# One inference step of a hybrid encoder layer: gate tiles before branch tiles, the convolution norm one tile up, and another order in the last block

## What is computed

```
hin = rmsnorm(x, g_pre_mix);  z = hin @ w_in
q, k, v, o_gate, it, lf = parts of z          # 4 heads of 256
hm = mLSTM(q, k, v, it, lf, C0, n0, m0)       # chunked matrix memory
hm = headnorm(hm) * g_headnorm * o_gate
branch_m = hm @ w_branch_m
u = z[CA] * sigmoid(z[CB]);  cv = depthwise_conv(concat(cache, u), 31 taps)
cv = silu(layernorm(cv, ln_g, ln_b))
branch_c = cv @ w_branch_c
merged = sigmoid(z[GM]) * branch_m + sigmoid(z[GC]) * branch_c
x = x + rmsnorm(merged @ w_out, g_post_mix)
hf = square(relu(rmsnorm(x, g_pre_ffn) @ w_ff1)) @ w_ff2
x = x + rmsnorm(hf, g_post_ffn)
```

## Time and profile before

| | |
|---|---|
| median of 3 runs (lowest to highest) | 1232.36 us (1231.77 to 1232.42) |
| profiled execution: time, span | 1232.35 us, 1230.5 us |
| mean granted clock of PE | 0.991 |
| busy: PE, DVE, ACT, POOL | 1194.1, 858.1, 450.4, 22.7 us |
| read from and written to HBM | 106.13 MB, 16.83 MB |

### The profile page before, as it was taken

One profiled execution on the slowest core, in us unless ns is written; L12 is line 12 of the kernel. 1 busy time (PEld: TensorE's weight loads), 2 busy tenths in 40 slices (PEclk: granted clock), 3 DMA queues, 4 the chain that ended last, 5 costly groups with the idle time before them and its releaser, 6 DMA issues.

```text
span 1230.5 us, 19269 instructions
## 1 busy us (share of the span) xinstructions
PE 1194.1 (97%) x7512; PEld 1117.4 (91%) x7512; DVE 858.1 (70%) x1522; ACT 450.4 (37%) x667; POOL 22.7 (2%) x37
## 2 busy tenths in 40 slices
PE   8999999999999999899999999979999999999996
PEld 7998999999999988899999998778998989899895
DVE  5644469888897989788655554986666666666667
ACT  5442243124323322312147223443525336254352
POOL 2000000000000000200000000000000000000000
PEclk9999999999999999999999999989999999999998
DMA  8342352353227223322322226122313231332323
GB/s 239 108 109 83 102 156 69 104 142 94 68 86 192 60 85 93 103 70 73 86 67 68 69 73 235 69 92 97 100 56 121 69 120 38 118 120 69 103 94 130
DMA packets 147834, 123.97 MB, mean 101 GB/s; under 512 B 13615, under 2 KB 131591, under 8 KB 147762
## 3 DMA queue, kind: packets, MB, share of 16 engines
q1 hardware_dynamic: 125138, 99.03, 27.4%
q10 hardware_dynamic: 22624, 23.95, 5.9%
HBM read 106.13 MB, written 16.83 MB: 100 GB/s over the span
## 4 chain that ended last, share of the span: by engine, by line
PE 82%; DVE 10%; ACT 3%; issue 2%; DMA 1%; SPq 0%; ACTq 0%; DVEq 0%; POOLq 0%; POOL 0%
PE out L417 39%; PE out L2310 16%; PE bank L2349 9%; PE out L2349 6%; PE bank L1998 5%; DVE CV L1252 4%; PE bank L1993 3%; PE out L2260 2%; PE bank L2260 2%; DVE WK L1252 2%; DVE WL L346 1%; DVE WK L1249 1%; DMA WK<-in_x_prompt 1%; DMA xend<-in_g_post_ffn 1%; PE out L398 1%
## 5 line engine op out<-in xcount | busy, mean ns | idle before, releaser
L417 PE MATMUL out<-XH,WH 128*128 128x320 f32 (+1 forms) x1024 | 239.5, 315 | 0.0
L417 PE MATMUL out<-XL,WH 128*128 128x320 f32 (+1 forms) x1024 | 237.4, 313 | 0.0
L417 PE MATMUL out<-XH,WL 128*128 128x320 f32 (+1 forms) x1024 | 237.4, 313 | 0.0
L1252 DVE SCALAR_TENSOR_TENSOR CV<-WK,cwu,CV 128x512 f32<-128x512 f32 x480 | 226.4, 542 | 0.0
L417 PEld LDWEIGHTS out<-XH,WH 128*128 128x128 f32 x1024 | 171.4, 189 | 5.0 <-issue 4.8
L417 PEld LDWEIGHTS out<-XL,WH 128*128 128x128 f32 x1024 | 172.6, 188 | 1.8 <-issue 1.3
L417 PEld LDWEIGHTS out<-XH,WL 128*128 128x128 f32 x1024 | 172.1, 188 | 1.5 <-issue 1.3
L346 DVE TENSOR_TENSOR WL<-ST,WH 128x1024 fp32r<-128x1024 f32 x85 | 104.3, 1227 | 88.1 <-ACT WH L338 87.0
L338 ACT ACTIVATE WH<-ST 128x1024 fp32r<-128x1024 f32 x85 | 89.6, 1054 | 113.1 <-PE out L417 57.9
L768 ACT ACTIVATE WK<-out 128x640 f32<-128x640 f32 (+1 forms) x56 | 39.8, 710 | 215.8 <-PE out L417 214.4
L1249 DVE TENSOR_TENSOR WK<-out,WK 128x512 f32<-128x512 f32 (+3 forms) x82 | 44.8, 567 | 53.6 <-PE out L417 32.1
(11 more groups left out here) (252 smaller groups left out, 2137.1 us busy)
## 6 DMA issues: line engine op xcount, KB each, us to landing
ST<-in_w_in SPq DMA_DIRECT2D x65, 512.0 KB, 4.0
ST<-in_w_ff SPq DMA_DIRECT2D x32, 1024.0 KB, 5.2
WK<-in_state_mlstm_C ACTq DMA_DIRECT2D x32, 256.0 KB, 4.2
o_C_sample<-WK ACTq DMA_DIRECT2D x32, 256.0 KB, 2.7
WK<-in_x_prompt SPq DMA_DIRECT2D x8, 512.0 KB, 7.3
ST<-in_w_branch_m SPq DMA_DIRECT2D x8, 512.0 KB, 4.7
ST<-in_w_branch_c SPq DMA_DIRECT2D x8, 512.0 KB, 4.1
ST<-in_w_out SPq DMA_DIRECT2D x8, 512.0 KB, 3.6
```

What stands on the lines that cost most here:

```text
L417: last = pe.matmul(out[s][:, h, 0:H], w[:, s, kk, :], x[:, kk, h * H:(h + 1) * H], start=(m < 2), stop=(m >= len(ms) - 2))
L1252: return dve.scalar_tensor_tensor(o, x, s, y, op0, op1)
```

## The change

1. **Gates and branch m.** All eight gate tiles come first, then the eight branch tiles. The sigmoids go straight into MG (`sg` is gone), and DVE multiplies in place. `headnorm_out` moves to the middle of the third gate tile, `epilogue_gate` on DVE to the fourth, `epilogue_out` on ACT ahead of the fourth evacuation, `u_out` behind the fifth tile. The taps are five per gate tile from the second on, then four per branch tile. The last two additions of the channel sum (`lsum`) go from the first GC tile to the last branch tile. SP's loads follow; that of the second gate tile waits for one low part more, that of the third for none of its own.
2. **Convolution norm.** Each of its steps stands one tile earlier among the GC tiles: mean at r = 0, subtraction 1, squares 2, sums 3, spread and multiplication 4, Silu 5 and 6.
3. **Last block.** ACT makes both high parts of the last unit (31) ahead of the squares of the last tile f, and DVE its low parts between the last sums. `gpf` has its place in WK (that of `x2q`) and is loaded when the squares of x2 are done, ahead of the wait for p3. DVE waits for x2 by group, in `y_final`. PE does parts 0 and 1 ahead for three groups only.

```diff
-    sg = wk(off["kt"], 2 * T2).rearrange("p (a t) -> p a t", a=2)
...
-    gpf, ysq = xend[:, 0:D], xend[:, D:D + 512]
+    ysq = xend[:, D:D + 512]
...
+    gpf = x2q
@@ -603,18 +603,16 @@
-            def gates_and_branch(i):
-                for r, (w, o) in enumerate(((w_in, OFF_GM), (w_in, OFF_GM + P), (w_m, 0), (w_m, P))):
-                    more = 0 if isinstance(i, int) else {1: 1, 2: -1}.get(r, 0)
-                    load_tile(sp, N(N_GM0, 4, i) + r, w, 0, i * 2 * P + o, more)
-
-            gates_and_branch(0)
+            for r in range(4):
+                load_tile(sp, N(N_GM0 + r), w_in, 0, OFF_GM + r * P, {1: 1, 2: -1}.get(r, 0))
...
-            with sp.Fori(1, KT // 2) as i:
-                gates_and_branch(i)
+            for r in range(4, KT):
+                load_tile(sp, N(N_GM0 + r), w_in, 0, OFF_GM + r * P)
+            for r in range(KT):
+                load_tile(sp, N(N_GM0 + KT + r), w_m, 0, r * P)
@@ -661,11 +659,12 @@
+            sp.wait_ge(sem("fsq"), 5)
+            dma(gpf, a["g_post_ffn"].to_broadcast([P, D]), "gpf")
 
             products(sp, 2 * NBLK - 1, "p3")
             for c in range(5):
-                dma(x2r[:, c, :], d_x2[:, c, :], "x2_in")
-            dma(gpf, a["g_post_ffn"].to_broadcast([P, D]), "gpf")
+                dma(x2r[:, c, :], d_x2[:, c, :], f"xagain{c if c else SMP}")
@@ -989,50 +988,46 @@
-            def gates_m(i):
-                n = N(N_GM0, 8, i)
-                for g in range(2):
-                    for r in range(2):
-                        hi(n + (4 * g + r + 1))
-                        if i or g:
-                            evacuated(act, n + (4 * g - 2 + r))
-                        evac(n + (4 * g + r), two(sg[:, r, :]), ACT.Sigmoid)
-                        if i == g == r == 0:
-                            epilogue_root(HEADS - 1)
-                    hi(n + (4 * g + 3))
-                    if i == g == 0:
-                        epilogue_out(HEADS - 1)
-                    hi(n + (4 * g + 4))
-                    if i == g == 0:
-                        u_rows(HEADS - 1)
-
-            gates_m(0)
-            gates_m(1)
+            for r in range(KT):
+                hi(N(N_GM0 + r + 1))
+                if r == 3:
+                    epilogue_out(HEADS - 1)
+                if r == 4:
+                    act.wait_ge(sem("hm_lo"), HEADS)
+                if r == 5:
+                    u_rows(HEADS - 1)
+                if r == 6:
+                    act.wait_ge(sem("u_out"), 48 * HEADS)
+                evac(N(N_GM0 + r), two(MG[:, r, :]), ACT.Sigmoid)
+                if r == 0:
+                    epilogue_root(HEADS - 1)
+            for r in range(KT):
+                hi(N(N_GM0 + KT + r + 1))
...
-            act.wait_ge(sem("u_out"), 16 * 3 * HEADS)
+            act.wait_ge(sem("np_out"), 16 * HEADS)
             for r in range(KT):
                 hi(N(N_GC0 + r + 1))
-                if r == 5:
+                if r == 4:
...
-                if r == 3:
+                if r == 2:
...
-                if r >= 6:
-
-                    for kk in range(4 * (r - 6), 4 * (r - 5)):
+                if r in (5, 6):
+
+                    for kk in range(4 * (r - 5), 4 * (r - 4)):
...
-                if r == 1:
+                if r == 0:
@@ -1074,7 +1069,10 @@
             def y_hi(u, t):
 
                 raw_in(act, u)
-                w_free(act, u, "a")
+                if u == NU - 1:
+                    products(act, f_of(u - 2), "p5" if t else "p2")
+                else:
+                    w_free(act, u, "a")
@@ -1198,13 +1196,17 @@
                 y_hi(u + 1, 0)
                 p5_copy(f)
                 y_hi(u + 1, 1)
+                if b == NBLK - 1:
+                    y_hi(u + 2, 0)
+                    y_hi(u + 2, 1)
                 row1(f)
...
                 row0(2 * b + 1)
-                y_hi(u + 1, 0)
-                y_hi(u + 1, 1)
+                if b < NBLK - 1:
+                    y_hi(u + 1, 0)
+                    y_hi(u + 1, 1)
@@ -1610,18 +1612,22 @@
                     epilogue_norm(HEADS - 1)
                 if j == 1:
                     unit_params(HEADS - 1)
+                    dve.wait_ge(sem("cache_in"), 32 * HEADS)
+                if j == 3:
                     epilogue_gate(HEADS - 1)
-                    dve.wait_ge(sem("cache_in"), 32 * HEADS)
-                if j == 10:
-                    dve.wait_ge(sem("u_out"), 48 * HEADS)
-                if j % 4 >= 2:
-                    kk = 2 * (j // 4) + j % 2
+                if j >= KT:
+                    r = j - KT
                     dve.wait_ge(sem("tile_done"), val(n) + 1)
-                    evacuated(dve, n + -2)
-                    tt(two(MG[:, kk, :]), gout(n), two(sg[:, j % 2, :]), ALU.mult
+                    evacuated(dve, N(N_GM0 + r))
+                    tt(two(MG[:, r, :]), gout(n), two(MG[:, r, :]), ALU.mult
                        ).then_inc(sem(f"of{n.par % 2}"), 1)
                 if j >= 1:
-                    t = taps(HEADS - 1, t, t + 5)
+                    t = taps(HEADS - 1, t, t + (5 if j < KT else 4))
+                if j == 2 * KT - 1:
+                    dve.wait_ge(sem("conv"), 2 * TAPS * HEADS)
+                    dve.wait_ge(sem("csum"), KT - 3)
+                    V.link(tt(ln[0], ln[0], CV[:, KT - 2, :], ALU.add))
+                    tt(ln[0], ln[0], CV[:, KT - 1, :], ALU.add).then_inc(sem("lsum"), 1)
@@ -1632,16 +1638,11 @@
-                if r == 0:
-                    dve.wait_ge(sem("conv"), 2 * TAPS * HEADS)
-                    dve.wait_ge(sem("csum"), KT - 3)
-                    V.link(tt(ln[0], ln[0], CV[:, KT - 2, :], ALU.add))
-                    tt(ln[0], ln[0], CV[:, KT - 1, :], ALU.add).then_inc(sem("lsum"), 1)
-                if r == 2:
+                if r == 1:
...
-                if r == 3:
+                if r == 2:
...
-                if r == 5:
+                if r == 4:
...
-                if r >= 6:
-                    conv_remainders(4 * (r - 6), 4 * (r - 5))
+                if r in (5, 6):
+                    conv_remainders(4 * (r - 5), 4 * (r - 4))
@@ -1915,13 +1916,18 @@
+                if b == NBLK - 1:
+                    y_lo(u + 1, 0)
+                    c12(f)
+                    y_lo(u + 1, 1)
+                    g_lo(f, 1)
+                    g_lo(f, 0)
+                    return
                 c12(f)
                 g_lo(f, 1)
                 g_lo(f, 0)
                 y_lo(u + 1, 0)
                 y_lo(u + 1, 1)
-                if b == NBLK - 1:
-                    return
@@ -1961,6 +1967,7 @@
                 dve.wait_ge(sem("yg"), 2 * x + 2)
+                dve.wait_ge(sem(f"xagain{x if x else SMP}"), 32)
...
             dve.wait_ge(sem("gpf"), 16)
-            dve.wait_ge(sem("x2_in"), 16 * 5)
@@ -2211,12 +2217,13 @@
             for j in range(2 * KT):
-                if j % 4 < 2:
-                    gemm(pe, N(N_GM0 + j), XH2, XL2, gaps=[lambda: headnorm_out(HEADS - 1)] if j == 1 else ())
+                if j < KT:
+                    gemm(pe, N(N_GM0 + j), XH2, XL2, gaps=[lambda: headnorm_out(HEADS - 1)] if j == 2 else ())
                 else:
-                    gemm(pe, N(N_GM0 + j), GH, GL, rhs_ready=(lambda kk: kk == 6 and pe.wait_ge(sem("hm_lo"), HEADS))
-                         if j == 2 else None)
-                if j == 2:
+                    if j == KT:
+                        pe.wait_ge(sem("hm_lo"), HEADS)
+                    gemm(pe, N(N_GM0 + j), GH, GL)
+                if j == 4:
                     u_out(HEADS - 1, N(N_HEADS0 + PER_HEAD * (HEADS - 1)))
@@ -2240,11 +2247,11 @@
-                gemm(pe, N(N_GC0 + r), XH2, XL2, gaps=[lambda: spread("lrt", "t_lr")] if r == 5 else ())
-                if r == 1:
+                gemm(pe, N(N_GC0 + r), XH2, XL2, gaps=[lambda: spread("lrt", "t_lr")] if r == 4 else ())
+                if r == 0:
...
-                if r == 4:
+                if r == 3:
@@ -2417,10 +2424,10 @@
-            for x in range(5):
+            for x in range(3):
                 y_last(x, 0, (0, 1))
             for x in range(5):
-                y_last(x, 0, (2, 3))
+                y_last(x, 0, (2, 3) if x < 3 else range(KH))
                 y_last(x, 1, range(KH))
```

## The result

| | before | after |
|---|---|---|
| median of the runs | 1231.95 us (6 runs, 1230.7 to 1232.42) | 1224.84 us (6 runs, 1223.1 to 1226.22) |
| profiled execution, its span | 1232.35, 1230.5 us | 1225.81, 1224.0 us |
| mean granted clock of PE | 0.991 | 0.990 |

The ratio is 0.9944, with an interval of 0.9934 to 0.9954: 7 us less. The prediction said 1225.4, in a range of 1223.2 to 1228.8.

The account below looks back on a forecast made before the run. PE, busy for 97% of the span, was taken as the bound, so only its waits and the end after its last matmul could give time: 1232.35 - 4.3 (gates) - 0 (norm) - 2.6 (last block) = 1225.4 us, range 1223.2 to 1228.8.

Parts of the forecast that it names:

- Gates: Gate and branch tiles: PE's waits for normalised heads, GL and WL go, 4.3 us less; bounds 1.2 to 4.3.
- the walk: Gate and branch tiles: the three queues followed with profiled durations; tightest, the sixth tile's low part, near 526.5, wanted at 528.4.
- 1.2 + 0.7 + 2.4: PE's waits in us: second gate tile, first branch tile, ahead of the second branch tile; all 4.3 were to go.
- Norm: Convolution norm one tile up: gains nothing, because ACT's unchanged chain and the low part wanted at its end both move a tile.
- single WL wait of 3.1 to 3.4 us: Sign of being right, in the convolution norm: PE waits once for a weight tile's low part, with no GL wait.
- The rival in which it goes: Convolution norm: its wait goes after all, saving 3 us and 1.8 of clock, 1220.6 us; chance 0.04.
- Clock: Behind the convolution norm's wait: PE's spell at 1.2 GHz stays, costing 1.8 us over seven tiles.
- 2.4 us before 519.11: Idle of PE ahead of the second branch tile that left the clock at 1.00; cited for the clock not falling.
- the clock doesn't fall: Behind the convolution norm's wait: no fall to 1.2 GHz, or a lesser one, worth 1.8 us, 1223.6 us; chance 0.17.
- Last block: End of the span: DVE's second addition of group 0 starts earlier, PE then bounds by half a microsecond; 2.6 us less.
- The lower bound of 0.9 us: Last block's least gain: what lay in DVE's wait for the norm's vector alone.
- The slower rival: Eight branch tiles: DVE becomes the bound if its work takes over 7.04 us a tile, counted 5.8; 1235 us; chance 0.02.

Follow-up runs that it names:

- the filling: Changed kernel plus 14 matmuls whose output nobody reads, ahead of the first tile of the last branch where PE stands: 1222.53 us, ratio 0.9919.
- the vector alone: Kernel before with the norm's vector issued ahead of the last products and x2 waited for by group, nothing else: 1230.75 us, ratio 0.9992, end 60.8 us.
- pairs: Kernel before with two of early vector, early unit-31 weight parts, new PE order: ratios 0.9994 (vector, parts), 0.9992 (vector, order), 1.0003 (parts, order).
- all three: Kernel before with only the last block's edit: early vector, early last-unit weight parts and PE's new order: 1229.25 us, ratio 0.9983, end 59.0 us.

## Why the prediction was right

**Gates: -4.3 predicted, -5.1 measured.** The mechanism is as walked: no wait for heads, GL or WL before 600 us; the tight low part was done at 526.46 where the walk had 526.5, wanted at 528.2 where it had 528.4 (a margin of 1.7 us, 1.4 low parts, and not the "nearly two" of the prediction); DVE takes 5.7 us of a branch tile of 7.03 (the walk 5.8). The term was sized from waits alone, 1.2 + 0.7 + 2.4. Each wait also costs PE's pipelining: its last matmuls otherwise overlap the next by 0.16 us (records of 0.31 or 0.46 us that start every 0.15 or 0.29), and the first pair behind a wait takes 0.56 instead of 0.46 (the last two rows of the timeline with the filling). That is 0.27 us a wait, 0.8 for three, and 4.3 + 0.8 = 5.1.

**Norm: 0 predicted, 0 in its stretch.** 55.82 and 55.83 us. The reason holds: the end of the wait is set by ACT's chain, which moved with the tile that needs it. The predicted single WL wait of 3.1 to 3.4 us is 3.4. The rival in which it goes is out.

**Clock: kept at 1.8 predicted, 3.0 measured in the profile.** This is the step that failed in size. I wrote "I keep it: the idle gets longer, not shorter", and took the one value that the trace of before had. The runs show that it isn't one value: nothing, 1.5 or some 2.7 us behind the old waits (over the tiles at full clock in the same experiments; my 3.0 and 1.8 are over 7.03 a tile), and 2.5 to 2.7 in both profiles with the single wait. The argument that 2.4 us before 519.11 brought no fall was one draw too; three other executions had it there. The rival "the clock doesn't fall" had it right that the outcome varies, but in the profiled execution it went the other way. Nor did I allow for the clock at the start, which moves a profile by 1.0 to 2.5 us.

**Last block: -2.6 predicted, -2.55 measured.** Point by point: second addition of group 0 8.6 us behind the products (8.6), groups at 4.66 (1202.90 to 1207.56), PE standing 0.2 us for the gated rows (0.1 to 0.2), DVE waiting 0.44 us for PE before the last group (half a microsecond), last addition at 1217.40, 27.8 us behind the products (1221.3 - 1193.5 = 27.8). The lower bound of 0.9 us was the vector alone, and this is what that experiment gave: 0.75 in the stretch.

**The sum.** 0.8 more in the gates and 1.2 less by the clock nearly cancel: 1225.4 predicted, 1225.81 in the profiled execution, 1224.84 the median. The agreement is closer than the steps deserve. The base is a draw too: 31 runs of the kernel before lie at 1230.3 to 1230.9 (15 runs, mean granted clock 0.992), 1231.8 to 1232.5 (13, 0.990 or 0.991) and 1234.5 to 1234.7 (3, 0.988), and the 1232.35 that I summed from is of the middle group. The slower rival (DVE bound in the branch tiles) would have needed over 7.03 us; DVE waits 1.38 us for PE in each of them behind the first.

## What to carry to other kernels

Ask of a wait that shall go away whether the chain that ends it gets shorter or only moves: moving the norm with its consumer gave 0, taking three table loads out of it 6.35 us (2.67 of them a slow clock that not every execution has). Price a wait of PE with its refilling (0.27 us here) and with the slow clock that may follow (0 to 2.8 us from run to run for the same waits), and read each edit in its own stretch between landmarks, since this scatter is as large as the edits. Where several things hold an engine within a microsecond of each other, test them together: here pairs gave 0, 0.8 and 1.2 us, all three 2.55.

## What the runs showed of the hardware

A wait of PE of 2.2 to 2.4 us was followed by 1.2 GHz in some executions and by none in others, in kernels alike up to this place and in it; the price, where it came, was 1.5 or 2.6 to 2.8 us of PE's time. Waits of 0.79 and 1.2 us near the start were followed by it in eleven profiles of fourteen, at 1.0 to 1.5 or 2.3 to 2.5 us. With 14 idle-filling matmuls in a wait of 3.4 us the clock stayed at 2.4 GHz in the profiled execution, and the median fell by 2.3 us though the wait ended no sooner. A table load of ACT took 1.28 us, with the next instruction 0.02 us behind.
